# Decode attention: transposed probabilities of two kv groups as the stationary operand of the values product, a pipeline one step deeper, and one turn of the output at the end

## The reference

```
s_c = q . k_cmp * scale + bias          (32 compressed keys)
s_s = q . k_sel * scale + bias          (512 past keys and the new ones)
s_w = q . k_win * scale + bias          (512 window keys and the new ones)
p   = softmax_masked(s)                 (one for each of the three)
o   = g0 * p_c @ v_cmp + g1 * p_s @ v_sel + g2 * p_w @ v_win
mix = o.reshape(..., 16 * 64) @ o_w
```

## Time and profile before

| what | before |
|---|---|
| runs, median (lowest to highest) | 2373.39 us (2372.66 to 2379.29) |
| the profiled execution, its span | 2372.5 us |
| PE busy | 2189.5 us (92%) |
| DVE, ACT, POOL busy | 849.7, 652.3, 860.4 us |
| dense projections L1122 in the chain that ended last | 47% |
| the loop over the 8 sequences | from 1688.6 to 1837.8 us of the span |

### The profile page before, as it was taken

The page is one execution under the profiler, slowest core; times in us unless marked ns, Lnnn a source line. Parts: engine busy times, 40 slices in busy tenths (PEclk is TensorE's granted clock), DMA queues, the critical chain, the costliest instruction groups (busy, mean ns, idle before and its releaser), DMA issues.

```text
span 2372.5 us, 37626 instructions
## 1 busy us (share of the span) xinstructions
PE 2189.5 (92%) x15160; PEld 1989.3 (84%) x15160; DVE 849.7 (36%) x1839; ACT 652.3 (27%) x1105; POOL 860.4 (36%) x528
## 2 busy tenths in 40 slices
PE   7999999969879999999999997999899989999996
PEld 6988888859679999999899995665567979999995
DVE  7474747564332200121221216655321342002213
ACT  3442424322123211221231304433211242112212
POOL 2444444455246513553443230000000345435531
PEclk9998989889899989999999898999966989999998
DMA  4112112131221243222213331000442112222221
GB/s 159 65 50 104 52 63 81 45 127 47 87 71 62 81 102 103 80 83 86 97 54 140 107 90 54 1 1 1 137 165 72 62 45 80 80 80 80 80 84 54
DMA packets 53394, 184.57 MB, mean 78 GB/s; under 512 B 7070, under 2 KB 11838, under 8 KB 50720
## 3 DMA queue, kind: packets, MB, share of 16 engines
q1 hardware_dynamic: 41424, 138.05, 17.7%
q0 software_dynamic: 9568, 41.69, 4.9%
q10 hardware_dynamic: 2288, 3.23, 0.4%
HBM read 158.20 MB, written 27.28 MB: 78 GB/s over the span
## 4 chain that ended last, share of the span: by engine, by line
PE 73%; DVE 12%; issue 7%; ACT 4%; POOL 3%; ACTq 0%; DMA 0%; POOLq 0%; DVEq 0%
PE dense L1122 47%; PE dense L1375 3%; PE bS L1228 2%; PE bS L1293 2%; PE bM L1459 2%; DVE tile L1591 1%; PE dense L1411 1%; PE dense L1474 1%; POOL split L622 1%; PE bX L1459 1%; PE bS L1197 1%; DVE tile L1654 1%; POOL xs L715 1%; PE bS L1411 1%; PE dense L1532 1%
## 5 line engine op out<-in xcount | busy, mean ns | idle before, releaser
L1122 PE MATMUL dense<-xs,split 128*128 128x288 f32 x6848 | 986.4, 302 | 41.1 <-POOL xs L715 21.9
L1122 PEld LDWEIGHTS dense<-xs,split 128*128 128x128 f32 x6848 | 953.2, 193 | 57.1 <-issue 46.8
L622 POOL TENSOR_TENSOR split<-ring,split 128x1024 fp32r<-128x1024 f32 x212 | 543.4, 2564 | 892.1 <-ACT split L833 892.1
L833 ACT ACTIVATE split<-ring 128x1024 fp32r<-128x1024 f32 x212 | 225.0, 1061 | 894.8 <-PE dense L1122 880.3
L1122 PE MATMUL dense<-hid,split 128*128 128x288 f32 x3072 | 420.3, 299 | 5.8 <-POOL split L622 5.8
L1122 PEld LDWEIGHTS dense<-hid,split 128*128 128x128 f32 x3072 | 419.5, 192 | 6.1 <-POOL split L622 6.1
L1603 DVE SCALAR_TENSOR_TENSOR tile<-tile,dense 128x576 f32 (+1 forms) x56 | 42.2, 754 | 491.2 <-PE dense L1122 491.2
L1746 DVE TENSOR_SCALAR sq<-dense 128x576 f32<-128x576 f32 x64 | 48.5, 758 | 320.5 <-PE dense L1122 314.4
L808 POOL DMA_DIRECT2D o_win<-tile x8 | 4.6, 571 | 375.4 <-DMA tile<-in_win 375.4
L726 POOL TENSOR_TENSOR hid<-sq,hid 128x576 f32 x64 | 76.8, 1201 | 0.0
L1591 DVE SCALAR_TENSOR_TENSOR tile<-tile,tile,tile 128x512 f32<-128x512 f32 x72 | 71.8, 997 | 2.6
(11 more groups left out here) (301 smaller groups left out, 2530.0 us busy)
## 6 DMA issues: line engine op xcount, KB each, us to landing
ring<-in_w SPq DMA_DIRECT2D x212, 512.0 KB, 3.2
tile<-in_state POOLq DMA_DIRECT2D x4, 2048.0 KB, 9.4
o_sssm<-tile POOLq DMA_DIRECT2D x4, 2048.0 KB, 7.5
tile<-in_cmp POOLq DMA_DIRECT2D x32, 256.0 KB, 3.3
tile<-in_sel SPq DMA_DIRECT2D x32, 256.0 KB, 3.0
tile<-in_win SPq DMA_DIRECT2D x8, 1024.0 KB, 7.3
o_win<-tile POOLq DMA_DIRECT2D x8, 1024.0 KB, 4.2
o_kv<-tile POOLq DMA_DIRECT2D x1, 3456.0 KB, 12.7
```

The source lines that it names most:

```text
L622: pool.tensor_tensor(split[:, j, 1, :], ring[:, j, :], split[:, j, 0, :].bitcast(F32), ALU.subtract).then_inc(w_split, 1)
L833: act.activation(split[:, j, 0, :], ring[:, j, :], ACT.Copy).then_inc(w_hi, 1)
L1122: mm = pe.matmul(dense[:, 2 * par + h_, 0:HT], split[:, j, w, cols], v[:, kk, h_ * HT:(h_ + 1) * HT], start=kk == 0 and t == 0, stop=kk == ...
```

## The change

1. In V(b) the operands change places. Stationary is now a block of 64 columns of the transposed probabilities (two kv groups), moving are the 128 value columns of these two groups. A product gives a 64 by 128 result whose two off-diagonal quarters are not used. There are 22 products for a sequence instead of 44, the two pairs `pr` alternate, and they write partitions 0 to 63 and 64 to 127.
2. S(b) is written so that the two `gp` alternate as well.
3. The results of all sequences stay in PSUM (`new_out`): 4 in `bDn[:, 0]`, 4 in `bS[:, 1]`. After the loop they are copied to `Od`, turned by 8 transposes, and put into `qT` by four strided copies. The copy to `qT` per sequence (L1085) is gone.
4. `PTd` and `PTs` are double, and the order on TensorE becomes S(0), then for each b: S(b+1), V(b-1), T(b), and V(7) at the end. On ScalarE the exponentials of b+1 come ahead of the copies of b.

```
         pe.wait_ge(npt_act, b + 1)
         pe.wait_ge(npt_dve, b + 1)
-        if b:
-            pe.wait_ge(no_ready, b)
-        for g in range(NKV):
-            o_ = bDn[half_of(g), 0, (g // 2) * 32:(g // 2) * 32 + 32]
-            vs = slice(256 + g * HD, 256 + (g + 1) * HD)
-            for pg in range(NPG):
-                k0 = pg * P + 32 * g
-                pe.matmul(o_, skv[b % KVB][:, pg, vs], PTd[:, k0:k0 + 32], start=pg == 0, stop=False)
-                pe.matmul(o_, wkv[b % KVB][:, pg, vs], PTd[:, PAST + k0:PAST + k0 + 32], start=False, stop=False)
...
+        o_ = [new_out(b)[64 * pr:64 * pr + 64, :] for pr in range(2)]
+        for pg in range(NPG):
+            for kv, probs in ((skv[b % KVB], PTd[b % 2][0]), (wkv[b % KVB], PTd[b % 2][1])):
+                for pr in range(2):
+                    k0 = pg * P + 64 * pr
+                    pe.matmul(o_[pr], probs[:, k0:k0 + 64], kv[:, pg, 256 + pr * P:256 + (pr + 1) * P],
+                              start=pg == 0 and kv is skv[b % KVB], stop=False)
...
+    new_scores(0)
+    for b in range(NB):
+        if b + 1 < NB:
+            new_scores(b + 1)
+        if b:
+            new_values(b - 1)
+        new_transposes(b)
+    new_values(NB - 1)
+
+    pe.wait_ge(nsc_read, NB)
+    pe.wait_ge(od_act, 1)
+    for b in range(NB):
+        if b == 4:
+            pe.wait_ge(od_dve, 1)
+        mm = pe.transpose(dense[:, b // 4, (b % 4) * P:(b % 4 + 1) * P], Od[:, b, :], ident[:, :])
+    mm.then_inc(ot_done, 1)
...
+    for bank, kv in ((bD[0], skv[b % KVB]), (bD[1], wkv[b % KVB])):
+        for gp in range(2):
+            pe.matmul(bank[rows[gp], :], qn[:, gp, b, :], kv[:, :, gp * P:(gp + 1) * P],
+                      start=True, stop=True)
...
 (scalar)
+        if b + 1 < NB:
+            new_exps(b + 1)
+        act.wait_ge(ntp_done, b + 1)
+        if b >= 2:
+            act.wait_ge(no_done, b - 1)
+        act.activation(PTd[b % 2][0], bX[:, :], ACT.Copy)
...
+    act.wait_ge(no_done, 4)
+    act.activation(Od[:, 0:4, :].rearrange("p b x -> p (b x)"), bDn[:, 0, :], ACT.Copy).then_inc(od_act, 1)
+    act.wait_ge(ot_done, 1)
+    for gp in range(2):
+        act.activation(new_out_rows(0, gp), new_out_by_feature(0, gp), ACT.Copy).then_inc(no_ready, 1)
...
 (vector)
+    dve.wait_ge(no_done, NB)
+    dve.tensor_copy(Od[:, 4:8, :].rearrange("p b x -> p (b x)"), bS[:, 1, :]).then_inc(od_dve, 1)
+    dve.wait_ge(ot_done, 1)
+    for gp in range(2):
+        dve.tensor_copy(new_out_rows(1, gp), new_out_by_feature(1, gp)).then_inc(no_ready, 1)
```

More of the change, by code:

```diff
@@ L259, in build @@
         Pd = [carve(2 * (PAST + ND) + NCMP) for _ in range(2)]
-        PTd = carve(2 * PAST)
-        PTs = carve(3 * P)
+        Od = carve(NB, P)
         assert at[0] <= xs_at + 2 * GR * NP_TOK
+        at[0] = xs_at + 2 * GR * NP_TOK + 2 * NPG * 512
+        PTs = [carve(3 * P) for _ in range(2)]
+        assert at[0] <= xs_end
+        PTd = [[PT[2 * i + k] for k in range(2)] for i in range(2)]
         ptab = sb("ptab", [1, NB * NPG], I32)
@@ L422, in build @@
         no_done = sem("new_o_summed")
+        od_act = sem("new_o_kept_a")
+        od_dve = sem("new_o_kept_b")
+        ot_done = sem("new_o_transposed")
         no_ready = sem("new_o_ready")
@@ L519, in build, with new_out, new_out_by_feature, new_out_rows @@
         TILES = [(g, c, g * NT + c) for g in range(MG) for c in range(NT)]
+        def new_out(b):
+            return (bDn[:, 0, :], bS[:, 1, :])[b // 4][:, (b % 4) * P:(b % 4 + 1) * P]
+        def new_out_by_feature(h_, gp):
+            src = dense[half_of(h_), 0:2, :].rearrange("p k (b x) -> p (k b) x", x=P)
+            c0 = (2 * gp + h_) * GR * NS
+            return src[:, :, c0:c0 + GR * NS].rearrange("p b (r i) -> p r b i", r=GR)
+        def new_out_rows(h_, gp):
+            return qT[half_of(h_), gp * GR:(gp + 1) * GR, NP_TOK:T].rearrange("p r (b i) -> p r b i", b=NB)
         def raw_new(j):
@@ L1492, in new_scores @@
                     pe.wait_ge(nsc_read, b)
-                for gp in range(2):
[L1494 to L1501, removed]
+                rows = [slice(64 * gp, 64 * gp + 64) for gp in range(2)]
+                for bank, kv in ((bD[0], skv[b % KVB]), (bD[1], wkv[b % KVB])):
+                    for gp in range(2):
+                        pe.matmul(bank[rows[gp], :], qn[:, gp, b, :], kv[:, :, gp * P:(gp + 1) * P],
+                                  start=True, stop=True)
+                for br in range(2):
+                    for gp in range(2):
+                        pe.matmul(bS[rows[gp], 0, br * ND:(br + 1) * ND], qn[:, gp, b, :],
+                                  kvT[:, 4 * (br + 1) + gp, NP_TOK:T], start=True, stop=True)
+                for gp in range(2):
+                    mm = pe.matmul(bS[rows[gp], 0, 2 * ND:2 * ND + NCMP], qn[:, gp, b, :], kc[:, b, gp, :],
+                                   start=True, stop=True)
                 mm.then_inc(nsc_done, 1)
@@ L1507, in _, with new_transposes @@
             W = PAST + ND
[L1508 to L1511, removed]
+            def new_transposes(b):
                 p_ = Pd[b % 2]
                 pe.wait_ge(npn_ready, b + 1)
+                if b:
+                    pe.wait_ge(npt_act, b)
+                    pe.wait_ge(npt_dve, b)
                 for pg in range(NPG):
@@ L1520, in _, with new_values @@
                 pe.transpose(bDn[0:NCMP, 1, 2 * P:3 * P], p_[:, 2 * W:2 * W + NCMP], ident[:, :]).then_inc(ntp_done, 1)
+            def new_values(b):
                 pe.wait_ge(npt_act, b + 1)
                 pe.wait_ge(npt_dve, b + 1)
-                if b:
-                    pe.wait_ge(no_ready, b)
-                for g in range(NKV):
-                    o_ = bDn[half_of(g), 0, (g // 2) * 32:(g // 2) * 32 + 32]
-                    rows = slice(32 * g, 32 * g + 32)
-                    vs = slice(256 + g * HD, 256 + (g + 1) * HD)
-                    for pg in range(NPG):
-                        k0 = pg * P + 32 * g
-                        pe.matmul(o_, skv[b % KVB][:, pg, vs], PTd[:, k0:k0 + 32], start=pg == 0, stop=False)
-                        pe.matmul(o_, wkv[b % KVB][:, pg, vs], PTd[:, PAST + k0:PAST + k0 + 32], start=False, stop=False)
-                    for br in range(2):
-                        pe.matmul(o_, Vt[0:ND, 4, br, g, :], PTs[0:ND, br * P + 32 * g:br * P + 32 * g + 32],
+                o_ = [new_out(b)[64 * pr:64 * pr + 64, :] for pr in range(2)]
[5 more added lines that the diff above has]
+                                      start=pg == 0 and kv is skv[b % KVB], stop=False)
+                for br in range(2):
+                    for pr in range(2):
+                        k0 = br * P + 64 * pr
+                        pe.matmul(o_[pr], PTs[b % 2][0:ND, k0:k0 + 64],
+                                  Vt[0:ND, 4, br, 2 * pr:2 * pr + 2, :].rearrange("p g d -> p (g d)"),
@@ L1536, in _ @@
                                   start=False, stop=False)
-                    mm = pe.matmul(o_, vc[0:NCMP, b, g, :], PTs[0:NCMP, 2 * P + 32 * g:2 * P + 32 * g + 32],
+                for pr in range(2):
+                    k0 = 2 * P + 64 * pr
+                    mm = pe.matmul(o_[pr], PTs[b % 2][0:NCMP, k0:k0 + 64],
+                                   vc[0:NCMP, b, 2 * pr:2 * pr + 2, :].rearrange("p g d -> p (g d)"),
                                    start=False, stop=True)
                 mm.then_inc(no_done, 1)
+            new_scores(0)
@@ L1960, in _ @@
                 dve.wait_ge(ntp_done, b + 1)
-                dve.tensor_copy(PTd[:, PAST:2 * PAST], bM[:, :]).then_inc(npt_dve, 1)
+                if b >= 2:
+                    dve.wait_ge(no_done, b - 1)
+                dve.tensor_copy(PTd[b % 2][1], bM[:, :]).then_inc(npt_dve, 1)
+            dve.wait_ge(no_done, NB)
+            dve.tensor_copy(Od[:, 4:8, :].rearrange("p b x -> p (b x)"), bS[:, 1, :]).then_inc(od_dve, 1)
+            dve.wait_ge(ot_done, 1)
+            for gp in range(2):
+                dve.tensor_copy(new_out_rows(1, gp), new_out_by_feature(1, gp)).then_inc(no_ready, 1)
             windows_stored(dve)
```

15 lines of the change are left out of this document (5 added, 10 removed).

## The result

The changed kernel takes 2340.45 us (median of 4 runs, 2339.3 to 2347.69), the kernel before, on the same chips, 2374.81 us (2372.66 to 2379.29). The ratio is 0.9861 with a 95% interval from 0.9842 to 0.988: 1.4% faster, 33 us (28 to 38).

What follows compares the result with a forecast made beforehand. PE was taken as the bound before, a ring of load, S and V after: 1708 + 5 x 19.7 + 17.6 = 1824.1 us against 1837.8, so 2372.5 - 13.7 + 0.9 = 2359.7 us; range 2346 to 2376 us.

Steps and rivals of the forecast that it cites:

- The ring: In the loop, sequences 3 to 7: load, S(s), V(s-2), next load form a closed cycle, 19.7 us a turn.
- load does not hold the loop: Rival for the whole loop: products save all they promise, 7.5 us a sequence, 2298 us; chance 0.04.
- no overlap: Rival for scores and values: alternating passes don't overlap, a turn is 23.8 us, 2389 us, slower; chance 0.10.
- turns: Sign in the trace after: starts of scores lie 19 to 21 us apart.
- the 9 named: Sign in the trace after: PE idles 9 to 11 us before each of the scores of sequences 3 to 7.
- the pair at 1.2 passes: Scores and values: two passes on alternating output partitions cost 1.2 passes, not 2; values 3.6 us at full clock.
- full-overlap rival: Rival for scores and values: pairs cost one pass, scores 2.1, values 3.0, a turn 18.8 us, 2354 us; chance 0.14.
- the pass at 0.136 us: Values: a pass of 128 columns costs at most 0.136 us at full clock, a switch of the array's shape included.
- S and V of a turn: Scores and values in one turn: 4.3 us at half clock, 0.35 us of scores left, 3.6 us values: 8.2 us.
- the clock's price in head and end: Head and end of the loop: 2 us added to each for a possible loss of PE's clock.
- the load: Rows for sequences 3 to 7: 0.74 us to issue plus 10.8 us from first issue to store, 11.5 us a turn.
- The three parts: Loop cut into head, five turns and end: forecast 19.4, 98.5 and 17.6 us.

## Why the prediction was wrong, point by point

**Right.** The ring was named before the run: TensorE waits for the rows ahead of the scores of sequences 3 to 7, and DMA releases it. A load is issued 0.82 us after a V in four cases of five and 1.16 us in the third, VectorE and ScalarE are no matter. The new order was called a loss against the products' gain, and the runs with the old order and with a fourth slot show it. The rivals "load does not hold the loop" and "no overlap" both fell. So the mechanism held, and what failed are terms of the sum. Of the signs named beforehand those of size failed with them: turns of 16.9 to 20.0 us from scores to scores where 19 to 21 were named, and two waits of 8.8 and 8.9 us below the 9 named.

**Wrong in size: the pair at 1.2 passes.** This is the step that failed most: on the prediction's own account (2359.7 against 2354 us for its full-overlap rival) it is worth 5.7 us. The prediction took the 0.26 us between the starts of the two passes of a pair for a rate, against 0.215 us alone. It had only that first step after a wait. In the scores the first step after a wait is 0.45 us and the others 0.43 us each, with one half as with two, so a start-up cost is paid once and a pair costs one pass. That start-up is 0.02 us there and the 0.26 us hold 0.045; the difference stays unexplained. The Trainium skill's "up to 2x" for tiles of 64 columns (TensorEngine Tiling (Array Packing), Theoretical Speedup), which the prediction put aside for that row, agrees with what the changed kernel shows: 1.74 us for eight passes of 0.43 us.

**Wrong in size: the pass at 0.136 us.** It had the array's change of shape spread over eight passes, and I charged it to all 44. Passes of 128 columns stand 0.109 us apart, 22 steps make 2.4 us, and the start and two changes of shape add 0.4 us: 2.8 us, where full overlap at 0.136 us gives 3.0 us and the forecast was 3.6. This term alone is 0.2 us a sequence. Scores take 3.8 us, mostly at half clock, forecast 4.65; the clock is back some 3.9 us after they begin, forecast 4.3. S and V of a turn are 6.83 us on average, forecast 8.2: 6.9 us in five turns, and 1.5 us more in the end's two V. The full-overlap rival had nearly these sizes and still came out 14 us too long, since it kept the steps below.

**Wrong: the clock's price in head and end.** I added 2 us in each, because TensorE idles there. The windows have 1.00 in both. In the kernel before the clock fell within the old values, although TensorE had no gap there. Of the 10 us of V(1) they are these 8.5:

```profile
1721.10:1729.60 8.50, 8.50 (x68) 7.86 (x68) 1.45 (x6) 0.00 (x0) 0.53 (x1) 0.50 0.31 130
```

The new values at full clock are over in 2.8 us. In the fourth-slot kernel with the old order the clock is 1.00 over five sequences, with a wait for the copies in each. What of this is due to the new operands and what to the shorter pieces, no run separates.

**Wrong in size: the load.** From V to S 10.95 us on average, 11.5 forecast: 2.7 us in five turns. The middle of longest and shortest was no bad guess for the kernel before, whose five loads average 10.74 us. Here they average 10.30 us from first issue to store, and TensorE goes on 0.24 us before the store is issued, which the forecast had counted as load.

The three parts come to 17.6 us: 3.5 in the head, 9.6 in the turns, 4.5 in the end. An estimate from the figures above puts 5.7 us of it down to the pair, 4 to the clock's price, 2.7 to the load, and the rest to the pass, the earlier return of the clock and transposes with copies of 2.5 us instead of 2.84. The other 1.7 us to the forecast lie outside the loop, which begins 1.2 us earlier after than before, though nothing there was edited. In the other kernels of this document with three slots, whose TensorE code ahead of the loop is the same, it begins between 1686.4 and 1691.0, so that is scatter. All errors went one way, since each doubtful price was taken at its dear end, and the range around the sum did not take that in.

Two sentences of the prediction need a word. It said that TensorE takes its instructions in order. The experiments on the order of products show starts out of order between the halves. Past the waiting scores they don't reach: the copies for V(1) are done by 1706.1, and V(1) begins behind S(3) all the same, at 1717.47. And it counted on the overlap because the passes alternate, where four passes of a half in a row do as well.

## What to carry to other kernels

Before an order on the engine that frees a buffer is made deeper, count what lies between the instruction that frees it and the one that wants it full again: here that fell from a sequence of 18 us to the transposes of one sequence, 1.4 us, and 47.6 us of waits came in. One more buffer, or the shallow order with a wait of 1.5 us, was worth more than the hidden copy. And fp32 products that fill half of the output partitions should stand so that the halves take turns within four passes.

## What the runs showed that was not expected

- TensorE starts a pass that writes the other half of the output partitions ahead of up to four unfinished passes of the program, and runs the two at full rate side by side. With four in a row per half nothing is lost (2.00 against 1.97 us for 32 passes), with eight 0.54 us more, with sixteen 1.4 us.
- Idle time alone did not decide the granted clock here. It fell to 0.50 in the old values, in which TensorE had no gap, and stayed at 1.00 over five sequences in which TensorE was idle for a fifth of the time (32.23 of 40.0 us busy).
- A load of the same 2 MB with nothing beside it takes 9.4 to 11.4 us from first issue to the scores that it releases, in one run.
- What an edit saves on TensorE can be more than its own passes: with shorter scores the untouched values got more of the full clock, 5.5 us in five sequences.
